# RWKV loop: a block's products split by what they need, POOL's later masks behind them, decay sums in halves of the array

## Chip, cores and metric

One core of a Trainium2 chip runs the whole program. The metric is the device time of one execution in microseconds (us), the median of several.

## What is computed

Two transformer blocks on 512 tokens of width 1024. The second block mixes tokens with differential attention and with a two-directional RWKV recurrence of 8 heads of 64 channels; the change is in that recurrence alone:

```python
def rwkv_scan(r, decay, k, v, kk, a, s0, reverse):
    def step(S, inp):
        r_t, w_t, k_t, v_t, kk_t, b_t = inp            # b = kk * a
        sa = jnp.einsum('bhvk,bhk->bhv', S, kk_t)
        S = (S * w_t[:, :, None, :] - sa[..., None] * b_t[:, :, None, :]
             + v_t[..., None] * k_t[:, :, None, :])
        return S, jnp.einsum('bhvk,bhk->bhv', S, r_t)
...
decay = jnp.exp(-jnp.exp(w))
a = jax.nn.sigmoid((a0 + al @ a2).astype(jnp.float32))
k_dir = k * (1.0 + (a - 1.0) * p['k_a'])
```

It runs over 256 context tokens and then 512 tokens, forwards and backwards.

## The kernel before

The recurrence is done in chunks of 64 tokens: 12 chunks (`NCH`), of which the first 4 are context (`main(n)` is true from chunk 4). Both directions go together; a tile has 128 partitions, that is two heads of 64 channels (`HEADS` are the two row halves), four such pairs per direction. Two chunks make a block of 128 tokens (6 blocks). All matmuls are float32; the profile counts two records for each.

The order of work is written out by hand for each engine, with semaphores between them. The loop runs over iterations n = -1 to 12. In iteration n the triangular system of chunk n is inverted in five levels (`lv` 0 to 4), while the state of chunk m = n - 1 is finished and the Gram matrices of chunk g = n + 1 are made. A level is: T product on TensorE (`t_level`), copy by ScalarE, XY product on TensorE (`xy_level`), `update` on VectorE (line 3066), once per direction. Work of the other chunks stands between ("aside" work of `t_level`):

- level 0: `kv`; level 1: `gram_l`, `sa`, `gram_lt`, then VectorE's `x_init` and `y_init` (lines 3048 and 3051) and POOL's addition of the identity (line 3139);
- level 2: `outputs`, `new_state`, VectorE's `state` (lines 3071 and 3075);
- level 3: `gram` B, evacuated by VectorE to GB (line 3058); POOL makes five masked copies of GB from it, one per level (`loff`, line 3125), for the T products of the next iteration;
- level 4: `gram` K, evacuated to GK.

Blocks are prepared ahead, one direction at levels 3 and 4 each. Odd iterations make the rates (`latents` on TensorE, lines 2747 and 2749, sigmoids on ScalarE), even ones the sums of log decay (`cums`, line 2757, four matmuls of 128x256 with a mask "sums" that keeps the two chunks apart) and ScalarE's exponentials (`exps`). From these VectorE makes the operands of the next Gram matrices (`products`, lines 3034 to 3044) with one multiplication by POOL (`kka`, line 3118) among them. `products(b, 0)` stands at the end of an even iteration, `products(b, 1)` behind level 0 of the odd iteration that follows; `gram_l` of level 1 waits for both (`prods`). Block b is prepared in iteration n = 2b - 2, block 0 ahead of the loop.

Of the kernel before, what the change touches and what calls it, by code (L numbers as in the profile page):

```python
# [16 lines left out]
ALU = mybir.AluOpType  # L17
# [3 lines left out]
P = 128  # L21
# [2662 lines left out]
def rwkv_loop(k):  # L2684
# [17 lines left out]
    YF = v(A_MIX, KD, S)  # L2702
    ident = [k.ident[h, h] for h in HEADS]
    sems = {n: k.sem(f"rwkv_{n}") for n in (
        "latent_done", "rated", "cums_done", "exps", "k_gain", "kka", "prods", "gram_l", "gram_lt", "gram_b", "gram_k", "x_init", "y_init",
        "gb", "gk", "loff", "eye", "t_done", "t_copied", "xy_done", "xy", "turned", "tok_copied", "kv_done", "kv_copied",
        "sa_done", "sa_copied", "s_done", "state", "y_done", "y_copied")}
    flat = lambda ap: ap.rearrange("p a b -> p (a b)")
# [33 lines left out]
    def tensor(k, pe):  # L2742
# [9 lines left out]

        def cums(b, d):
            wait("rated", prep(b, d))
            for f in range(4):
                o = 2048 + 256 * f
                mm = pe.matmul(k.psum[:, o:o + 256], SIG[d][:, f * P:(f + 1) * P], mask(k, "sums", 0, 256), start=True, stop=True)  # L2757
            mm.then_inc(sems["cums_done"], 1)

        def prepare(n, d):  # L2760
# [161 lines left out]
        for n in range(-1, NCH + 1):  # L2922
            m, g, live = n - 1, n + 1, 0 <= n < NCH
            for lv in range(LEVELS):
                aside = nothing
                if lv == 1 and g < NCH:
                    aside = gram_l(g)
                elif lv == 2 and m >= 0:
                    aside = outputs(m)
                elif lv == 3 and g < NCH:  # L2930
                    aside = gram(g, B, "gram_b")
                elif lv == 4 and g < NCH:
                    aside = gram(g, K, "gram_k")
                if live:
                    t_level(n, lv, aside)
                rest(aside)
                if lv == 0 and m >= 0:
                    aside = turn_kb(m) if m < NCH - 1 else nothing
                    kv(m, n, aside)
                    rest(aside)  # L2940
                if lv == 1:
                    aside = turn_v(n) if live else nothing
                    if m >= 0:
                        sa(m, aside)
                    rest(aside)
                if lv == 4:
                    prepare(n, 1)
                if live:
                    xy_level(n, lv)
                if lv == 1 and g < NCH:  # L2950
                    gram_lt(g)
                if lv == 2 and 0 <= m < NCH - 1:
                    new_state(m, n)
                if lv == 3:
                    if n == -1:
                        wait("exps", 2)
                    prepare(n, 0)

    def scalar(k, act):
        wait = lambda name, value: act.wait_ge(sems[name], value)  # L2960
# [5 lines left out]

        def exps(b, d):
            wait("cums_done", prep(b, d))
            cum = k.psum[:, 2048:3072].rearrange("p (f w c t) -> p f w c t", f=4, w=2, c=2)
# [52 lines left out]
    def vector(k, dve):  # L3022
        wait = lambda name, value: dve.wait_ge(sems[name], value)

        def products(b, d):
            n, tok = b % 2, block_tokens(b, d)
            at_tokens = lambda name: src[name][:, :, tok].rearrange("p f (c t) -> p f c t", c=2)
            rate = RATE[d].rearrange("p (f t) -> p f t", f=4)
            Kf, Bf = (x[n][d].rearrange("p f c t -> p f (c t)") for x in (K, B))
            ka = M[:, O_VEC + VCOL["k_a_2"]:O_VEC + VCOL["k_a_2"] + 4].unsqueeze(2).broadcast_to([P, 4, 2 * CH])  # L3030
            wait("exps", prep(b, d))
            if b >= 2:
                wait("tok_copied", 3 * (2 * b - 2))
            ins = dve.scalar_tensor_tensor(out=Kf, in0=rate, scalar=-1.0, in1=ka, op0=ALU.add, op1=ALU.mult)
            ins.then_inc(sems["k_gain"], 1)
            tile = AR[n][d]
            dve.tensor_tensor(tile[:, :, :, 0, :], tile[:, :, :, 0, :], at_tokens("KK"), ALU.mult)
            if main(2 * b):
                dve.tensor_tensor(tile[:, :, :, 1, :], tile[:, :, :, 1, :], at_tokens("R"), ALU.mult)
            wait("k_gain", prep(b, d))  # L3040
            k.dve.link(dve.scalar_tensor_tensor(out=Kf, in0=Kf, scalar=1.0, in1=src["K"][:, :, tok], op0=ALU.add, op1=ALU.mult))
            k.dve.link(dve.tensor_tensor(Kf, Kf, Bf, ALU.mult))
            wait("kka", prep(b, d))
            dve.tensor_tensor(Bf, rate, Bf, ALU.mult).then_inc(sems["prods"], 1)  # L3044
# [31 lines left out]
            ins.then_inc(sems["state"], 1)  # L3076

        dve.memset(ST[0], 0.0).then_inc(sems["state"], 1)
        for d in range(2):
            products(0, d)  # L3080
        for n in range(-1, NCH + 1):
            m, g, live = n - 1, n + 1, 0 <= n < NCH
            for lv in range(LEVELS):
                if lv == 3 and g < NCH:
                    wait("gram_b", g + 1)
                    evacuate(g, GB, 0, 0)
# [8 lines left out]
                    evacuate(g, GK, 1, 1).then_inc(sems["gk"], 1)  # L3095
                if live:
                    update(n, lv, 1)
                if lv == 0 and n >= 1 and exps_in(n - 1) is not None:
                    products(exps_in(n - 1), 1)
                if lv == 1 and g < NCH:  # L3100
                    x_init(g)
                if lv == 2 and m >= 0 and main(m) and second_visit(m):
                    wait("y_done", m - NCH_CTX + 1)
                    for d in range(2):
# [2 lines left out]
                if lv == 2 and 0 <= m < NCH - 1:  # L3107
                    state(m)
            if exps_in(n) is not None:
                products(exps_in(n), 0)  # L3110

    def pool(k, pool):
        wait = lambda name, value: pool.wait_ge(sems[name], value)

        def kka(b, d):
            wait("k_gain", prep(b, d))
            rate = RATE[d].rearrange("p (f t) -> p f t", f=4)
            pool.tensor_tensor(rate, rate, src["KK"][:, :, block_tokens(b, d)], ALU.mult).then_inc(sems["kka"], 1)

        def loff(g, lv):  # L3120
            if lv == 0:
# [7 lines left out]
        for d in range(2):  # L3129
            kka(0, d)  # L3130
        for n in range(-1, NCH):
            g = n + 1
            if n >= 1 and exps_in(n - 1) is not None:
                kka(exps_in(n - 1), 1)
# [7 lines left out]
            if exps_in(n) is not None:  # L3142
                kka(exps_in(n), 0)

    return Phase("rwkv_loop", tensor=tensor, vector=vector, scalar=scalar, pool=pool)

# [288 lines left out]
```

## Time and profile before

| | |
|---|---|
| median of 3 runs | 2701.26 us (2696.73 to 2702.88) |
| profiled execution: its time, its span | 2695.02 us, 2693.1 us |
| TensorE matmul busy, weight load busy | 2495.5 us (93%), 1935.5 us (72%) |
| VectorE, ScalarE, POOL busy | 1337.9, 510.6, 160.1 us |
| loop, 1797 to 2169 us: TensorE, VectorE, ScalarE, POOL busy | 288.23, 187.04, 121.26, 122.13 us |
| mean granted clock in the loop, in the span | 0.94, 0.967 |

Times in the rows are us from the start of the span. The ends of iterations are taken at the end of VectorE's last update: iteration 6 ends at 2016.92, 7 at 2049.50, 8 at 2078.59, 9 at 2110.38, 10 at 2136.67. A granted clock of 1.00 is 2.4 GHz, 0.50 is 1.2 GHz.

### The profile page before, as it was taken

To read this page: it belongs to the slowest core of one execution; us is meant where nothing else is said; L and a number is where in the kernel's file an instruction comes from. 1 tells how busy PE (TensorE), PEld (TensorE's weight loads), DVE (VectorE), ACT (ScalarE), POOL (GpSimd) and SP (SyncE) were. 2 spreads that over 40 slices of the span, in tenths; PEclk is the share of its full clock that TensorE was granted. 3 is DMA by queue.
4 is the path that set the end of the run, shared out by engine and by line. 5 is a ranking of instruction groups with operands and counts; after the bars stand their busy time and mean duration, and the time that the engine had idled before them with its cause. 6 is when DMAs were issued, how large, how long until landed. Compare 5 with 4: busy or idle time off the path is not lost.

```text
span 2693.1 us, 49099 instructions
## 1 busy us (share of the span) xinstructions
PE 2495.5 (93%) x21464; PEld 1935.5 (72%) x21464; DVE 1337.9 (50%) x2466; ACT 510.6 (19%) x1032; POOL 160.1 (6%) x118
## 2 busy tenths in 40 slices
PE   8989999999999999999999989978877798999997
PEld 5945888888686448888884744547777746888886
DVE  4625555523444346555333274734555435777523
ACT  1121110001004320010001053223333222122100
POOL 0000000000000000000000000004333200000000
PEclk9988999999999999999999989989999998999998
DMA  4323222234120032222333103100000023222132
GB/s 163 120 76 125 94 93 69 70 86 122 56 89 30 1 125 67 91 94 75 82 110 116 46 16 84 32 1 4 4 4 4 4 94 107 82 94 94 50 90 65
DMA packets 221182, 190.54 MB, mean 71 GB/s; under 512 B 8727, under 2 KB 219064, under 8 KB 220968
## 3 DMA queue, kind: packets, MB, share of 16 engines
q1 hardware_dynamic: 220674, 187.29, 22.3%
q8 instruction: 171, 2.80, 0.4%
q14 instruction: 43, 0.35, 0.0%
q10 hardware_dynamic: 294, 0.09, 0.0%
HBM read 185.25 MB, written 2.10 MB: 70 GB/s over the span
## 4 chain that ended last, share of the span: by engine, by line
PE 86%; DVE 7%; issue 2%; ACT 2%; SPq 1%; DMA 1%; POOL 1%; DVEq 0%; POOLq 0%; ACTq 0%
PE psum L1630 30%; PE psum L1840 14%; PE psum L512 8%; PE psum L1130 4%; PE psum L2673 4%; PE psum L1344 3%; PE psum L2680 3%; PE psum L1341 3%; PE psum L3218 2%; PE psum L542 2%; PE psum L1066 1%; PE psum L2270 1%; PE psum L2757 1%; PE psum L2252 1%; DVE sbuf L3066 1%
## 5 line engine op out<-in xcount | busy, mean ns | idle before, releaser
L1630 PE MATMUL psum<-sbuf 128*128 128x256 f32 x3696 | 805.5, 381 | 3.6 <-ACT sbuf L488 1.7
L1630 PEld LDWEIGHTS psum<-sbuf 128*128 128x128 f32 x3696 | 707.0, 191 | 101.7 <-issue 3.1
L1840 PE MATMUL psum<-sbuf 128*128 128x256 f32 x1848 | 403.9, 381 | 11.1 <-DVE sbuf L1858 5.5
L1840 PEld LDWEIGHTS psum<-sbuf 128*128 128x128 f32 x1848 | 352.9, 191 | 61.8 <-DVE sbuf L1858 6.3
L1714 DVE TENSOR_TENSOR sbuf<-sbuf,psum 128x256 f32<-128x256 f32 x462 | 177.9, 417 | 201.2 <-PE psum L1630 200.0
L512 PE MATMUL psum<-sbuf 128*128 128x512 f32 (+3 forms) x688 | 247.9, 519 | 4.3 <-DVEq L617 4.0
L2680 PE MATMUL psum<-sbuf 64*64 64x64 f32 x4992 | 204.1, 231 | 30.0 <-issue 14.3
L2673 PE MATMUL psum<-sbuf 64*64 64x64 f32 (+1 forms) x4544 | 178.1, 232 | 48.7 <-DVE sbuf L3044 31.5
L512 PEld LDWEIGHTS psum<-sbuf 128*128 128x128 f32 (+2 forms) x688 | 129.4, 189 | 115.5 <-issue 103.4
L2680 PEld LDWEIGHTS psum<-sbuf 64*64 64x64 f32 x4992 | 179.3, 142 | 42.9 <-issue 34.8
L2673 PEld LDWEIGHTS psum<-sbuf 64*64 64x64 f32 x4544 | 162.8, 140 | 54.3 <-DVE sbuf L3044 32.7
L427 POOL TENSOR_TENSOR sbuf<-sbuf 128x512 f32<-128x512 f32 x30 | 37.8, 1279 | 1925.3 <-DVE sbuf L413 1925.1
L1876 DVE TENSOR_TENSOR sbuf<-sbuf,psum 128x256 f32<-128x256 f32 x84 | 34.2, 419 | 229.0 <-PE psum L1840 228.6
L3066 DVE TENSOR_TENSOR sbuf<-sbuf,psum 128x512 f32<-128x512 f32 (+1 forms) x120 | 73.5, 630 | 122.4 <-PE psum L2673 122.2
L1130 PE MATMUL psum<-sbuf 128*128 128x512 f32 x256 | 117.0, 607 | 0.0
L1650 ACT ACTIVATE sbuf<-sbuf 128x512 f32<-128x512 f32 x44 | 27.7, 630 | 399.7 <-DVE sbuf L1714 399.7
L1130 PEld LDWEIGHTS psum<-sbuf 128*128 128x128 f32 x256 | 48.0, 195 | 53.1 <-issue 53.1
L1344 PE MATMUL psum<-sbuf 128*128 128x256 f32 x392 | 85.4, 379 | 0.0
L1700 DVE TENSOR_TENSOR sbuf<-sbuf 128x512 f32<-128x512 f32 x66 | 44.5, 690 | 81.2 <-PE psum L1630 67.1
L1344 PEld LDWEIGHTS psum<-sbuf 128*128 128x128 f32 x392 | 74.2, 190 | 11.3 <-issue 1.3
L1178 DVE TENSOR_REDUCE sbuf<-psum 128x1 f32<-128x256 f32 (+3 forms) x80 | 36.8, 460 | 87.7 <-PE psum L1066 52.0
L3125 POOL TENSOR_TENSOR sbuf<-sbuf 128x512 f32<-128x512 f32 x60 | 74.2, 1273 | 67.9 <-DVE sbuf L3058 67.9
(280 smaller groups left out, 2719.5 us busy)
## 6 DMA issues: line engine op xcount, KB each, us to landing
sbuf<-in_w_mod_dram SPq DMA_DIRECT2D x24, 1024.0 KB, 5.2
sbuf<-in_w_ffn_gate_dram SPq DMA_DIRECT2D x22, 1024.0 KB, 5.3
sbuf<-in_w_ffn_up_dram SPq DMA_DIRECT2D x22, 1024.0 KB, 7.8
sbuf<-in_w_ffn_down_dram SPq DMA_DIRECT2D x32, 704.0 KB, 6.0
sbuf<-in_w_up_dram SPq DMA_DIRECT2D x22, 1024.0 KB, 7.0
sbuf<-in_w_out_dram SPq DMA_DIRECT2D x12, 1024.0 KB, 7.5
sbuf<-in_w_in_dram SPq DMA_DIRECT2D x12, 1024.0 KB, 5.4
sbuf<-in_w_down_dram SPq DMA_DIRECT2D x16, 704.0 KB, 6.1
```

The source lines that it names most:

```text
L512: mm = pe.matmul(bank, w[:, q, c0:c0 + m], rhs(k0 + q), start=start and q == 0, stop=stop and q == kc - 1)
L542: mm = pe.matmul(bank, act_chunk(q), w[:, q, :], start=q == 0, stop=q == kc - 1)
L1130: mm = pe.matmul(bank_of(b), tiles[b // 2][:, q, (b % 2) * P:(b % 2) * P + P], MIX[:, q, :], start=q == 0, stop=q == KD - 1)
L1341: mm = pe.matmul(self.bank(p)[:, t * P:(t + 1) * P], x[:, q, t * P:(t + 1) * P], w[:, q, :], start=q == 0, stop=q == 3)
L1344: mm = pe.matmul(self.bank(p), w[:, q, :], x[:, q, :], start=q == 0, stop=q == 3)
L1630: mm = pe.matmul(bank, w[:, q, :], rhs[:, q, :], start=q == 0, stop=q == 3)
L1714: dve.tensor_tensor(out, base, bank_of(u, p, t), ALU.add).then_inc(s["added"], 1)
L1840: mm = pe.matmul(bank_of(g, p), wt[:, q, :], rhs_of[p][:, q, :], start=q == 0, stop=q == UNITS - 1)
L2673: mm = pe.matmul(out[h], lhsT[h], rhs[h], start=start, stop=stop)
L2680: mm = pe.matmul(out[o], lhsT[h], rhs[h], start=start, stop=stop)
L3066: dve.tensor_tensor(xy, xy, new, ALU.subtract).then_inc(sems["xy"], 1)
L3125: pool.tensor_tensor(split(LOFF[lv]), split(GB[g % 2][:, :, 0, :]), both_level(lv), ALU.mult).then_inc(sems["loff"], 1)
```

## The change

- `cums` becomes eight matmuls: for each of four feature groups one per chunk, with the 64 rows of that chunk as contraction, into bank 4 for the first chunk and bank 5 for the second. ScalarE reads them in the new layout.
- TensorE's first `prepare` moves from behind the XY product of level 3 to ahead of it.
- `products` is split. `rate_products` (gain of the key, and the product of rate and KK that POOL made) goes to level 0 of the even iteration for both directions, `key_products` to level 1, the rest of the first direction to the head of level 4, the rest of the second to the end of the even iteration. Ahead of the loop, block 0's rate and key products stand before its exponentials are waited for.
- POOL no longer multiplies; its mask copies of levels 2 to 4 in an even iteration wait for the block's last product (`prods`).

```diff
         def cums(b, d):
             wait("rated", prep(b, d))
+            sums = mask(k, "sums", 0, 256).rearrange("p (w c t) -> p w c t", w=2, c=2)
             for f in range(4):
-                o = 2048 + 256 * f
-                mm = pe.matmul(k.psum[:, o:o + 256], SIG[d][:, f * P:(f + 1) * P], mask(k, "sums", 0, 256), start=True, stop=True)
+                for c, rows in enumerate(HEADS):
+                    mm = pe.matmul(k.bank[4 + c][:, f * P:(f + 1) * P], SIG[d][rows, f * P:(f + 1) * P], sums[rows, :, c, :],
+                                   start=True, stop=True)
             mm.then_inc(sems["cums_done"], 1)
...
+                if lv == 3:
+                    if n == -1:
+                        wait("exps", 2)
+                    prepare(n, 0)
                 if lv == 4:
                     prepare(n, 1)
                 if live:
...
-                if lv == 3:
-                    if n == -1:
-                        wait("exps", 2)
-                    prepare(n, 0)
...
-            wait("exps", prep(b, d))
             if b >= 2:
                 wait("tok_copied", 3 * (2 * b - 2))
-            ins = dve.scalar_tensor_tensor(out=Kf, in0=rate, scalar=-1.0, in1=ka, op0=ALU.add, op1=ALU.mult)
-            ins.then_inc(sems["k_gain"], 1)
-            tile = AR[n][d]
+            for d in range(2):
+                rate, Kf, _ = of_block(b, d)
+                wait("rated", prep(b, d))
+                dve.scalar_tensor_tensor(out=Kf, in0=rate, scalar=-1.0, in1=ka, op0=ALU.add, op1=ALU.mult).then_inc(sems["k_gain"], 1)
+            for d in range(2):
+                rate, _, _ = of_block(b, d)
+                wait("k_gain", prep(b, d))
+                dve.tensor_tensor(rate, rate, src["KK"][:, :, block_tokens(b, d)], ALU.mult).then_inc(sems["kka"], 1)
+
+        def key_products(b):
+            for d in range(2):
+                _, Kf, _ = of_block(b, d)
+                wait("k_gain", prep(b, d))
+                dve.scalar_tensor_tensor(out=Kf, in0=Kf, scalar=1.0, in1=src["K"][:, :, block_tokens(b, d)], op0=ALU.add,
+                                         op1=ALU.mult).then_inc(sems["k_made"], 1)
+
+        def products(b, d):
...
+            wait("exps", prep(b, d))
             dve.tensor_tensor(tile[:, :, :, 0, :], tile[:, :, :, 0, :], at_tokens("KK"), ALU.mult)
             if main(2 * b):
                 dve.tensor_tensor(tile[:, :, :, 1, :], tile[:, :, :, 1, :], at_tokens("R"), ALU.mult)
-            wait("k_gain", prep(b, d))
-            k.dve.link(dve.scalar_tensor_tensor(out=Kf, in0=Kf, scalar=1.0, in1=src["K"][:, :, tok], op0=ALU.add, op1=ALU.mult))
+            wait("k_made", prep(b, d))
             k.dve.link(dve.tensor_tensor(Kf, Kf, Bf, ALU.mult))
             wait("kka", prep(b, d))
             dve.tensor_tensor(Bf, rate, Bf, ALU.mult).then_inc(sems["prods"], 1)
...
             for lv in range(LEVELS):
+                if lv == 4 and exps_in(n) is not None:
+                    products(exps_in(n), 0)
...
-                if lv == 0 and n >= 1 and exps_in(n - 1) is not None:
-                    products(exps_in(n - 1), 1)
+                if lv == 0 and exps_in(n) is not None:
+                    rate_products(exps_in(n))
                 if lv == 1 and g < NCH:
                     x_init(g)
+                if lv == 1 and exps_in(n) is not None:
+                    key_products(exps_in(n))
...
             if exps_in(n) is not None:
-                products(exps_in(n), 0)
+                products(exps_in(n), 1)
...
                 for lv in range(LEVELS):
+                    if lv == 2 and exps_in(n) is not None:
+                        wait("prods", prep(exps_in(n), 1))
                     loff(g, lv)
```

VectorE's row before, from the end of iteration 6 (level 4's evacuations and updates) to the level-1 update of iteration 7:

```order
1251 L3058 TENSOR_TENSOR sbuf<-psum,sbuf 128x512
1252 L3066 TENSOR_TENSOR sbuf<-sbuf,psum 128x256
1253 L3058 TENSOR_TENSOR sbuf<-psum,sbuf 128x512
1254 L3066 TENSOR_TENSOR sbuf<-sbuf,psum 128x256
1255 L3034 SCALAR_TENSOR_TENSOR sbuf<-sbuf 128x512
1256 L3037 TENSOR_TENSOR sbuf<-sbuf 128x8x64
1257 L3039 TENSOR_TENSOR sbuf<-sbuf 128x8x64
1258 L3041 SCALAR_TENSOR_TENSOR sbuf<-sbuf 128x512
1259 L3042 TENSOR_TENSOR sbuf<-sbuf 128x512
1260 L3044 TENSOR_TENSOR sbuf<-sbuf 128x512
1261 L3066 TENSOR_TENSOR sbuf<-sbuf,psum 128x2x256 x2
1262 L3034 SCALAR_TENSOR_TENSOR sbuf<-sbuf 128x512
```

The same place after the change, in whose numbering L3058 to L3064 are the four products, L3078 the evacuation and L3086 the update:

```order
1250 L3058 TENSOR_TENSOR sbuf<-sbuf 128x8x64
1251 L3060 TENSOR_TENSOR sbuf<-sbuf 128x8x64
1252 L3062 TENSOR_TENSOR sbuf<-sbuf 128x512
1253 L3064 TENSOR_TENSOR sbuf<-sbuf 128x512
1254 L3078 TENSOR_TENSOR sbuf<-psum,sbuf 128x512
1255 L3086 TENSOR_TENSOR sbuf<-sbuf,psum 128x256
1256 L3078 TENSOR_TENSOR sbuf<-psum,sbuf 128x512
1257 L3086 TENSOR_TENSOR sbuf<-sbuf,psum 128x256
1258 L3058 TENSOR_TENSOR sbuf<-sbuf 128x8x64
1259 L3060 TENSOR_TENSOR sbuf<-sbuf 128x8x64
1260 L3062 TENSOR_TENSOR sbuf<-sbuf 128x512
1261 L3064 TENSOR_TENSOR sbuf<-sbuf 128x512
```

Two sets of six between the updates have become one set of four ahead of level 4's evacuations and one of four behind its updates.

The rest of them stands in levels 0 to 1 of iteration 6 after the change (L3040 key gain, L3044 rate times KK, L3068 and L3071 the starts of X and Y, L3050 the key product):

```order
1236 L3086 TENSOR_TENSOR sbuf<-sbuf,psum 128x2x256 x2
1237 L3040 SCALAR_TENSOR_TENSOR sbuf<-sbuf 128x512 x2
1238 L3044 TENSOR_TENSOR sbuf<-sbuf 128x512 x2
1239 L3086 TENSOR_TENSOR sbuf<-sbuf,psum 128x2x256 x2
1240 L3068 TENSOR_TENSOR sbuf<-psum,sbuf 128x512
1241 L3071 TENSOR_TENSOR sbuf<-psum,sbuf 128x512
1242 L3050 SCALAR_TENSOR_TENSOR sbuf<-sbuf 128x512 x2
1243 L3086 TENSOR_TENSOR sbuf<-sbuf,psum 128x2x256 x2
```

Four instructions have come between the updates of level 0 and level 1, and two between the start of Y and the updates of level 2.

## Rows read from the trace of the kernel before

**Rows 1.** Waits in the loop: us in total, times, longest us.

```profile
PEld psum L2680 <- issue: 34.8, 50, 2.3
...
PE psum L2673 <- DVE sbuf L3044: 31.5, 6, 6.8
```

**Rows 2.** Stretches of iterations 7, 8, 9 and 10, one row each.

```profile
core 0: us, PE busy (x) PEld busy (x) DVE busy (x) ACT busy (x) POOL busy (x), PEclk, DMA share, GB/s
...
2016.92:2049.50 32.58, 24.64 (x948) 23.30 (x948) 20.84 (x32) 10.43 (x23) 10.68 (x8) 0.90 0.02 4
2049.50:2078.59 29.09, 24.77 (x944) 22.31 (x944) 11.12 (x21) 11.45 (x27) 9.67 (x7) 1.00 0.02 4
2078.59:2110.38 31.79, 23.01 (x928) 21.80 (x928) 21.29 (x34) 6.50 (x16) 9.58 (x7) 0.84 0.02 4
2110.38:2136.67 26.29, 21.18 (x928) 19.67 (x928) 11.68 (x21) 6.49 (x16) 8.55 (x7) 1.00 0.02 4
```

**Rows 3.** Timeline of VectorE, iteration 6's level 3 to iteration 7's level 1.

```profile
2007.59 0.69 DVE L3058 TENSOR_TENSOR sbuf<-psum,sbuf 128x512 f32<-128x512 f32 x1 [0.27 <-PE psum L2673]
...
2016.51 0.41 DVE L3066 TENSOR_TENSOR sbuf<-sbuf,psum 128x256 f32<-128x256 f32 x1
...
2018.04 1.76 DVE L3039 TENSOR_TENSOR sbuf<-sbuf 128x512 f32<-128x512 f32 x1
...
2021.16 0.69 DVE L3044 TENSOR_TENSOR sbuf<-sbuf 128x512 f32<-128x512 f32 x1
...
2027.29 0.69 DVE L3044 TENSOR_TENSOR sbuf<-sbuf 128x512 f32<-128x512 f32 x1
2032.61 1.44 DVE L3066 TENSOR_TENSOR sbuf<-sbuf,psum 128x512 f32<-128x512 f32 x2 [4.64 <-PE psum L2673]
```

**Rows 4.** Timeline of ScalarE around the first exponentials of iteration 6.

```profile
2007.81 1.28 ACT L2972 ACT_TABLE_LOAD   x1
2011.12 0.60 ACT L2972 ACTIVATE sbuf<-psum 128x512 f32<-128x512 f32 x1 [2.02 <-PE psum L2757]
```

**Rows 5.** Chain that ended last: latents of iteration 5, cums of iteration 6.

```profile
1980.60 0.31 PE psum L2747
...
1981.35 0.34 PE psum L2749 x3
...
2009.16 1.92 PE psum L2757 x8
...
2012.99 1.92 PE psum L2757 x8
```

**Rows 6.** Timeline of POOL: identity in iteration 0, masks and product in 6.

```profile
1828.41 2.37 POOL L3139 TENSOR_TENSOR sbuf<-sbuf 128x1024 f32<-128x1024 f32 x1 [4.29 <-DVE sbuf L3051]
...
2009.56 6.18 POOL L3125 TENSOR_TENSOR sbuf<-sbuf 128x512 f32<-128x512 f32 x5 [7.79 <-DVE sbuf L3058]
2017.60 1.65 POOL L3118 TENSOR_TENSOR sbuf<-sbuf 128x512 f32<-128x512 f32 x1 [1.87 <-DVE sbuf L3034]
```

**Rows 7.** Stretches of 2 us in iteration 7, columns as in rows 2.

```profile
2024.00:2026.00 2.00, 0.00 (x0) 0.00 (x0) 2.00 (x3) 0.00 (x0) 1.38 (x1) 1.00 0.00 0
...
2028.00:2030.00 2.00, 1.97 (x72) 1.97 (x76) 0.00 (x0) 0.51 (x2) 0.00 (x0) 0.50 0.03 8
```

**Rows 8.** Timeline of VectorE, level 2 of iteration 0; levels 0, 1, 2 of 8.

```profile
1829.17 1.38 DVE L3066 TENSOR_TENSOR sbuf<-sbuf,psum 128x512 f32<-128x512 f32 x2 [0.91 <-PE psum L2673]
...
2052.66 0.69 DVE L3066 TENSOR_TENSOR sbuf<-sbuf,psum 128x512 f32<-128x512 f32 x1 [3.15 <-PE psum L2673]
...
2058.38 1.29 DVE L3066 TENSOR_TENSOR sbuf<-sbuf,psum 128x512 f32<-128x512 f32 x2 [3.45 <-PE psum L2673]
...
2064.81 1.28 DVE L3066 TENSOR_TENSOR sbuf<-sbuf,psum 128x512 f32<-128x512 f32 x2 [3.94 <-PE psum L2673]
```

**Rows 9.** Start of the loop, timelines of VectorE and of TensorE.

```profile
1802.29 0.69 DVE L3034 SCALAR_TENSOR_TENSOR sbuf<-sbuf 128x512 f32<-128x512 f32 x1 [10.90 <-ACT sbuf L2976]
...
1811.09 1.65 PE L2673 MATMUL psum<-sbuf 64*64 64x64 f32 x26 [6.78 <-DVE sbuf L3044]
```

More of the change, by code:

```diff
@@ L2704, in rwkv_loop @@
     sems = {n: k.sem(f"rwkv_{n}") for n in (
-        "latent_done", "rated", "cums_done", "exps", "k_gain", "kka", "prods", "gram_l", "gram_lt", "gram_b", "gram_k", "x_init", "y_init",
+        "latent_done", "rated", "cums_done", "exps", "k_gain", "kka", "k_made", "prods", "gram_l", "gram_lt", "gram_b", "gram_k", "x_init", "y_init",
         "gb", "gk", "loff", "eye", "t_done", "t_copied", "xy_done", "xy", "turned", "tok_copied", "kv_done", "kv_copied",
@@ L2968, in exps @@
             wait("cums_done", prep(b, d))
-            cum = k.psum[:, 2048:3072].rearrange("p (f w c t) -> p f w c t", f=4, w=2, c=2)
+            cum = k.psum[:, 2048:3072].rearrange("p (c f w t) -> p f w c t", c=2, f=4, w=2)
             incl, excl = cum[:, :, 0], cum[:, :, 1]
@@ L3023, in vector, with of_block, rate_products @@
         wait = lambda name, value: dve.wait_ge(sems[name], value)
-        def products(b, d):
-            n, tok = b % 2, block_tokens(b, d)
-            at_tokens = lambda name: src[name][:, :, tok].rearrange("p f (c t) -> p f c t", c=2)
+        def of_block(b, d):
+            n = b % 2
             rate = RATE[d].rearrange("p (f t) -> p f t", f=4)
             Kf, Bf = (x[n][d].rearrange("p f c t -> p f (c t)") for x in (K, B))
+            return rate, Kf, Bf
+        def rate_products(b):
             ka = M[:, O_VEC + VCOL["k_a_2"]:O_VEC + VCOL["k_a_2"] + 4].unsqueeze(2).broadcast_to([P, 4, 2 * CH])
-            wait("exps", prep(b, d))
             if b >= 2:
                 wait("tok_copied", 3 * (2 * b - 2))
-            ins = dve.scalar_tensor_tensor(out=Kf, in0=rate, scalar=-1.0, in1=ka, op0=ALU.add, op1=ALU.mult)
-            ins.then_inc(sems["k_gain"], 1)
-            tile = AR[n][d]
+            for d in range(2):
[13 more added lines that the diff above has]
+        def products(b, d):
+            rate, Kf, Bf = of_block(b, d)
+            at_tokens = lambda name: src[name][:, :, block_tokens(b, d)].rearrange("p f (c t) -> p f c t", c=2)
+            tile = AR[b % 2][d]
+            wait("exps", prep(b, d))
             dve.tensor_tensor(tile[:, :, :, 0, :], tile[:, :, :, 0, :], at_tokens("KK"), ALU.mult)
@@ L3078, in vector @@
         dve.memset(ST[0], 0.0).then_inc(sems["state"], 1)
+        rate_products(0)
+        key_products(0)
         for d in range(2):
@@ L3109, in vector @@
             if exps_in(n) is not None:
-                products(exps_in(n), 0)
+                products(exps_in(n), 1)
     def pool(k, pool):
         wait = lambda name, value: pool.wait_ge(sems[name], value)
[L3115 to L3118, printed above, removed]
         def loff(g, lv):
@@ L3128, in pool @@
             [P, 2, 4, CH])
-        for d in range(2):
-            kka(0, d)
         for n in range(-1, NCH):
             g = n + 1
-            if n >= 1 and exps_in(n - 1) is not None:
-                kka(exps_in(n - 1), 1)
             if g < NCH:
```

2 lines of the change are left out of this document (removed).

## Prediction

> **What bounds the kernel now.** I first read the times and the page, then the waits of the RWKV loop, then one stretch per iteration, then the instructions of iterations 6 to 8 engine by engine. The loop is about 370 of 2695 us; the change touches nothing else, so all of the effect must come from there. In the loop no engine is full: TensorE and VectorE hand work to each other at every level (T product, ScalarE copy, XY product, VectorE update). Two waits stand out [rows 1]: TensorE waits six times for the last product of a block, 31.5 us in all, up to 6.8 us at once; and it stops for "issue" (nothing in the profile released it), 34.8 us on its weight-load side in 50 stops.
>
> The stretches show who pays [rows 2]. Iterations 7 and 9 (odd: a block's second set of products runs in them) take 32.58 and 31.79 us; iterations 8 and 10 take 29.09 and 26.29 us. Iterations 9 and 10 do the same work except for the products: 5.50 us apart. In iteration 6 VectorE ends the last update at 2016.92, then does block 4's first products until 2021.8, the next two updates, and the second products until 2027.98; the next XY update comes at 2032.61 [rows 3]. In iteration 8 the same three kinds of update come at 2052.66 and 2058.38 with VectorE idle 3.15 and 3.45 us before them [rows 8]. From the last update (iteration 7's ended at 2049.50, the boundary in [rows 2]) to the level-1 update it is 8.9 us there, and 15.7 us where the products stand between. The 6.8 us are two things: TensorE has nothing to do while VectorE multiplies, and its granted clock falls with it. It was 1.00 in 2024 to 2026 and 0.50 in 2028 to 2030, that is 1.2 instead of 2.4 GHz, after a stretch in which it did nothing [rows 7].
>
> **The change, part by part.**
>
> *Products taken out of the chain.* Per block and direction, before: six VectorE instructions (five in the two context blocks) and one on POOL. After: the two that need only the rate, with POOL's product now VectorE's, go to level 0 of the even iteration, the key product to level 1, the three or four that need the exponentials to level 4 (first direction) and behind it (second). VectorE spends 0.6 to 0.7 us on each.
>
> Odd iterations gain. What is left behind the last update is one direction's four products: 0.6+0.6+0.7+0.7 = 2.6 us, and POOL's masks of levels 2 to 4 are made to wait for them, so nothing holds the port. The idle time there is 3.15 us [rows 8], so it is covered; without cover each 0.6 us would lie on the path. Gain per odd iteration: 5.50 us from iterations 9 and 10. For iteration 7: iteration 8 has two cums of 1.92 us and iteration 7 two latents of 1.09 us (1980.60 to 1981.69) [rows 5], so a free iteration 7 should take 29.09 - 2 x 0.83 = 27.4, gain 5.2. I take 5.3 for all five odd iterations: -26.5. Bounds: nothing taken off for cums, (32.58-29.09 = 3.5) in four of them and 5.5 in the ninth: -19.5; the whole distance 15.7 - 8.9 in each: -34.
>
> *Rate and key products in gaps.* Four instructions, 2.5 us, against the 3.45 us of idle time behind level 0's updates: hidden from iteration 4 on. The two key products come right behind Y's start, just when POOL adds the identity (2.37 us in the row of iteration 0) [rows 6]. These collide: when POOL's 1.65 us product started at 2017.60, VectorE's instruction of 2018.04 took 1.76 instead of 0.69 us, and ended 0.55 us after POOL did [rows 3, 6]. So the second key product ends about 0.6+2.37+0.6 = 3.6 us after Y's start. In iteration 8 the next update is idle for 3.94 us: hidden. In iteration 0 it is idle for 0.91 us [rows 8]: first key product 1828.2 to 1828.9, POOL to 1831.25, second to 1831.8, so the update of 1829.17 moves by 2.6 us. With up to 0.7 for the rate products there (POOL is still at its masks) and 1.0 for iteration 2, where new_state on TensorE covers most: +4.3.
>
> *Level 3 and 4 of even iterations*, worked through for iteration 6. TensorE ends gram B at about 2007.6 (VectorE's row of 2007.59). Cums now stands here: the same 2048 columns, but in halves of 64 rows with a bank each. Latents, which already feed two separate row ranges into two banks, push 2 x 512 columns in one and 8 x 128 in the other in 1.09 us together, so they overlap; I take 1.0 instead of 1.92 (bounds 0.96 and 1.92). Then the XY product's first half (2008.95), update 0.65, GB evacuation 0.6, update 0.65: 2010.85. GB is whole at 2010.25, and gram K with the T product, 1.91 us between the two cums [rows 5], ends at 2012.2 instead of 2012.99; cums and XY product of level 4 end at 2013.8 instead of 2015.6. So TensorE is 1.8 us early. ScalarE: table load ends 2009.1 [rows 4], four exponentials 0.5 apart: 2010.8.
>
> VectorE gives this back. It now meets products(b, 0), four instructions, at 2010.85, ahead of GK's evacuation and both updates. POOL gets GB at 2010.3 and makes two masks of 1.24 us (6.18 for five [rows 6]). With two SBUF inputs VectorE waits for each as above: 2.6 us of work and 2 x 1.24 less the 0.5 already gone by: end 2015.3. Then evacuation 0.6, update 0.34, evacuation 0.6, update 0.41: 2017.3, against 2016.92 before. So +0.4 per even iteration, +2.0. Bounds: no collision, -1.5 each (-7.5); POOL's masks put between every pair cannot cost more, since only two are let through before the new wait.
>
> The Trainium skill bears on this (SBUF — State Buffer, Who interferes with whom): an instruction of VectorE with two SBUF inputs and a GpSimd instruction that reads SBUF never share the port pair; the later one waits for the whole of the other. By it the collision is certain; without it the last number would be 2015.5 instead of 2017.3. The rows of 2017.60 and 2018.04 agree.
>
> *POOL's new wait.* Behind it stand masks 2 to 4 (3.7 us). They start about 2.7 us after the last update and end at +6.4; the T product of level 2 needs the first of them after the level-1 update, at +8.9 at the earliest. Costs nothing; its cover is 2.5 us or more.
>
> *Start.* Before, products began only after the first exponentials, at 1802.29, and TensorE's gram waited 6.78 us for the tenth of them, until 1811.09 [rows 9]. Four of ten are now done while ScalarE and TensorE are still at the first sums, the first sums are 1.9 us shorter (at half clock), and no POOL instruction stands between (about 2 x 1.07): 1802.3 - 1.9 + 6 x 0.65 + 0.7 of waiting for the second exponentials gives 1805. Gain 6.
>
> **Sum.** -26.5 + 4.3 + 2.0 - 6.0 = -26.2 us on the profiled execution's 2695.02: 2668.8. That execution lies 6.2 us under the median of the runs shown (2701.26), so on the median's scale it is 2675; I give 2674.
>
> **Rivals.**
> 1. *The port costs nothing, or the odd iterations give the whole distance.* Even iterations then keep 1.5 us each (-7.5 for +2.0) and odd ones up to 6.8. Against: the 1.76 us row, and iteration 9 to 10, which gave 5.5 of its 6.7. Time 2650 to 2662. Chance 0.09.
> 2. *Issue stops take the freed time.* TensorE runs through an odd iteration at half clock for some 5 us now; at full clock it uses up instructions faster, and stops of about 0.7 us (34.8/50 [rows 1]) come more often. Three or four more per odd iteration: +2.5 each, +12.5. For: such stops stand in the fast iterations. Against: iteration 10 has them and is the measure I used. Time 2687. Chance 0.13. In a sentence of its own: the Trainium skill (Runtime: NRT & Kernel Launch, Instruction fetch mechanics) says that instructions are refilled in blocks of 256 ahead of use and that this is mostly hidden; by that this rival would be nothing.
> 3. *The clock falls in the new gap.* In level 4 of an even iteration TensorE is done at 2013.8 and VectorE delivers at 2016.3: 2.5 us with nothing to do. The clock fell after such a stretch in the odd iteration, where nothing ran in 2024 to 2026 [rows 7]. If it falls in each of five gaps and 5 us then run at half speed, +2.5 each: 2687. Chance 0.1.
> 4. *Slower.* The same fall, lasting: then the T product, the kv and sa products of the next iteration run at half clock and TensorE's next gaps keep it down. It turns the sign from 5.2 us lost per pair of iterations, 10.5 us at half clock; at 15 us of half clock it is +37 - 26 = 2712. Against: in all odd iterations so far the clock came back within some 6 us of steady work. Chance 0.04.
> 5. *Nothing to be measured*, for instance because the second products at the end of the even iteration still hold up the level-0 update and the early ones level 1 (2.6 us each time, 13) and rival 2 comes too: about 2699. Chance 0.04.
>
> The forecast, 2664 to 2684, has 0.6. The range 2659 to 2689 takes in rivals 2 and 3 and leaves out most of 1, and 4 and 5. A measurement of this kernel tells 0.2% (5.4 us): faster by more 0.91, within 0.04, slower 0.05.
>
> **What would show each step.** In odd iterations, the granted clock stays at 1.00 and TensorE no longer waits for the products' last line; the distance last update to level-1 update is about 9 us. Each cums takes about 1 us. In even iterations one or two of the four products at level 4 last 1.2 to 1.8 us instead of 0.7, and the evacuation of GK comes at the end of them. The second key product takes over 2 us, and only iterations 0 and 2 feel it. Iteration 7 takes 27.4, 9 takes 26.3, 6 about 30.6. The forecast is wrong if odd iterations stay above 29 us or even ones rise above 32.

## The result, and the profile after

| | before | after |
|---|---|---|
| median of 4 runs | 2699.24 us | 2676.47 us (2674.92 to 2680.07) |
| ratio | | 0.9923, 95% interval 0.9906 to 0.9939 |
| profiled execution: its time, its span | 2695.02, 2693.1 us | 2680.07, 2678.3 us |
| first latents to last update of iteration 11 | 368.9 us | 360.6 us |

A second comparison, with 5 runs of the change, gave 0.9930 (0.9918 to 0.9942). The change is faster by 0.7 to 0.8%, about 20 us; 2674 had been forecast, against 2676.5.

The stall that the change removes is gone from the iterations. The profile's stretches of iterations 7, 8, 9 and 10 after the change, cut as in [rows 2] at VectorE's last updates:

```profile
core 0: us, PE busy (x) PEld busy (x) DVE busy (x) ACT busy (x) POOL busy (x), PEclk, DMA share, GB/s
...
2008.01:2038.26 30.25, 23.33 (x948) 21.55 (x948) 13.71 (x23) 10.55 (x23) 11.13 (x9) 1.00 0.02 4
2038.26:2069.89 31.63, 23.75 (x960) 21.53 (x960) 21.07 (x30) 11.67 (x27) 6.75 (x4) 1.00 0.02 4
2069.89:2097.33 27.44, 21.00 (x928) 19.69 (x928) 14.26 (x26) 6.50 (x16) 10.01 (x8) 1.00 0.02 4
2097.33:2125.31 27.98, 22.50 (x928) 21.30 (x928) 11.78 (x21) 6.51 (x16) 8.56 (x7) 0.94 0.02 5
```

Iterations 7 and 9 have fallen from 32.58 and 31.79 us to 30.25 and 27.44, and the granted clock in them from 0.90 and 0.84 to 1.00. Iterations 8 and 10 are longer than in [rows 2], by 2.5 and 1.7 us; iteration 10 has no products and no sums, so nothing was edited in it. In the second profiles of both kernels (below) iteration 8 takes 30.7 us before and 30.3 after, so nothing of its excess is left; iteration 10 takes 27.1 and 28.9, the same difference again, and what lengthens it is open.

VectorE in iteration 6, from the level-1 updates to the level-1 update of iteration 7 (L3050 key products, L3078 evacuation, L3086 update, L3058 to L3064 the products that need exponentials), answers to [rows 3]:

```profile
1989.12 0.68 DVE L3071 TENSOR_TENSOR sbuf<-psum,sbuf 128x512 f32<-128x512 f32 x1
1989.72 3.44 DVE L3050 SCALAR_TENSOR_TENSOR sbuf<-sbuf 128x512 f32<-128x512 f32 x2
1993.09 0.68 DVE L3086 TENSOR_TENSOR sbuf<-sbuf,psum 128x512 f32<-128x512 f32 x1
...
1998.22 0.69 DVE L3078 TENSOR_TENSOR sbuf<-psum,sbuf 128x512 f32<-128x512 f32 x1 [0.43 <-PE psum L2673]
1999.96 0.69 DVE L3086 TENSOR_TENSOR sbuf<-sbuf,psum 128x512 f32<-128x512 f32 x1 [1.04 <-PE psum L2673]
...
2001.76 1.39 DVE L3058 TENSOR_TENSOR sbuf<-sbuf 128x512 f32<-128x512 f32 x1
2003.07 1.75 DVE L3060 TENSOR_TENSOR sbuf<-sbuf 128x512 f32<-128x512 f32 x1
2004.74 0.68 DVE L3062 TENSOR_TENSOR sbuf<-sbuf 128x512 f32<-128x512 f32 x1
2005.46 0.69 DVE L3064 TENSOR_TENSOR sbuf<-sbuf 128x512 f32<-128x512 f32 x1
2006.07 0.68 DVE L3078 TENSOR_TENSOR sbuf<-psum,sbuf 128x512 f32<-128x512 f32 x1
...
2007.60 0.41 DVE L3086 TENSOR_TENSOR sbuf<-sbuf,psum 128x256 f32<-128x256 f32 x1
...
2009.85 0.69 DVE L3064 TENSOR_TENSOR sbuf<-sbuf 128x512 f32<-128x512 f32 x1
2012.58 1.29 DVE L3086 TENSOR_TENSOR sbuf<-sbuf,psum 128x512 f32<-128x512 f32 x2 [2.04 <-PE psum L2673]
2017.52 0.69 DVE L3086 TENSOR_TENSOR sbuf<-sbuf,psum 128x512 f32<-128x512 f32 x1 [3.65 <-PE psum L2673]
```

Three things are to be seen. The last update of iteration 6 ends at 2008.01 and the level-1 update of iteration 7 comes at 2017.52, 9.5 us later instead of 15.7. At level 4 two of the four products are stretched, to 1.39 and 1.75 us, and the evacuation of GK waits for all four. The second key product waits for POOL's identity: 3.44 us for two. POOL's timeline at the same places:

```profile
1989.94 2.67 POOL L3156 TENSOR_TENSOR sbuf<-sbuf 128x1024 f32<-128x1024 f32 x1 [10.49 <-DVE sbuf L3071]
2001.33 2.95 POOL L3146 TENSOR_TENSOR sbuf<-sbuf 128x512 f32<-128x512 f32 x2 [8.71 <-DVE sbuf L3078]
```

The two masks take 2.95 us, where five took 6.18 [rows 6]: mask, product, mask, product. So the engines take turns, one instruction each, even though POOL's second mask was ready from the start.

What took part of the gain back is seen in TensorE's waits. First iteration 9 before (2078.59 to 2110.38), then iteration 9 after (2069.89 to 2097.33); the columns are us in total, times, longest us:

```profile
PE psum L2673 <- DVE sbuf L3044: 5.0, 1, 5.0
PE psum L2680 <- DVE sbuf L3066: 2.6, 4, 1.7
PE psum L2673 <- issue: 0.9, 2, 0.7
...
PE psum L2680 <- issue: 0.2, 1, 0.2
```

```profile
PE psum L2680 <- issue: 2.4, 2, 1.4
PE psum L2673 <- issue: 2.0, 3, 1.0
PE psum L2819 <- issue: 1.1, 1, 1.1
```

The wait of 5.0 us for the products is gone, and "issue" (stops in which TensorE waited for nothing that the profile shows) has gone from 1.1 to 5.5 us.

### The profile page after: what moved, and what is told of

The parts are those of the page before. It is cut to its first block, busy times and chain, and to the rows that moved or that the text cites. A ratio compares the mean times of both kernels' runs of the same rounds, so it can differ in the third digit from the quotient of the medians.

```text
span 2678.3 us, 49291 instructions
## 1 busy us (share of the span) xinstructions
PE 2486.2 (93%) x21560; PEld 1929.4 (72%) x21560; DVE 1350.4 (50%) x2478; ACT 512.7 (19%) x1032; POOL 144.5 (5%) x106
## 4 chain that ended last, share of the span: by engine, by line
PE 86%; DVE 6%; issue 3%; ACT 2%; SPq 1%; POOL 1%; DMA 0%; DVEq 0%; POOLq 0%; ACTq 0%
PE psum L1630 30%; PE psum L1840 14%; PE psum L512 8%; PE psum L1130 4%; PE psum L2680 4%; PE psum L2673 3%; PE psum L1344 3%; PE psum L1341 3%; PE psum L3235 2%; PE psum L542 2%; PE psum L1066 1%; DVE sbuf L3086 1%; PE psum L2270 1%; PE psum L2252 1%; PE psum L1109 1%
## 5 line engine op out<-in xcount | busy, mean ns | idle before, releaser
L2680 PEld LDWEIGHTS psum<-sbuf 64*64 64x64 f32 x4992 | 175.5, 139 | 62.7 <-issue 53.7
L2673 PE MATMUL psum<-sbuf 64*64 64x64 f32 (+1 forms) x4544 | 177.0, 230 | 21.7 <-issue 15.4
L2673 PEld LDWEIGHTS psum<-sbuf 64*64 64x64 f32 x4544 | 160.4, 138 | 28.0 <-issue 18.3
L3086 DVE TENSOR_TENSOR sbuf<-sbuf,psum 128x512 f32<-128x512 f32 (+1 forms) x120 | 73.1, 630 | 114.4 <-PE psum L2673 114.2
```

Of the source, the lines that this page charges most:

```text
L2673: mm = pe.matmul(out[h], lhsT[h], rhs[h], start=start, stop=stop)
L2680: mm = pe.matmul(out[o], lhsT[h], rhs[h], start=start, stop=stop)
L3086: dve.tensor_tensor(xy, xy, new, ALU.subtract).then_inc(sems["xy"], 1)
```

## Where the gain went: terms against two profiles of each kernel

Both kernels were profiled a second time (`c_before`, `c_after`). All entries are us. The two numbers under before and after are the two profiles of that kernel, and the difference is that of their means. Iterations are cut as above; "start" is from the first latents to the end of iteration 0.

| stretch | before | after | difference | forecast |
|---|---|---|---|---|
| start | 49.2, 49.7 | 51.9, 51.8 | +2.3 | -6.0 + 3.3 + 0.4 |
| odd iterations 1 to 9 | 158.0, 159.5 | 139.5, 138.2 | -19.9 | -26.5 |
| even iterations 2 to 8 | 112.6, 116.7 | 117.7, 116.4 | +2.5 | +1.0 + 1.6 |
| iterations 10 and 11 | 49.1, 51.1 | 51.6, 51.1 | +1.2 | 0 |
| loop | 368.9, 377.0 | 360.6, 357.4 | -13.9 | -26.2 |
| before and behind the loop | 2324.2, 2322.7 | 2317.7, 2316.9 | -6.2 | 0 |
| span | 2693.1, 2699.7 | 2678.3, 2674.3 | -20.1 | -26.2 |

Two profiles of one kernel differ by up to 4 us in a row (even iterations before), so differences of 1 or 2 us are not to be leaned on. The total came into the range partly by luck: the loop's gain was overestimated by 12 us, and 6 us outside of it, which had not been forecast, made up half of that.

## Experiments

**Second profiles.** Nothing edited.

> The kernel before, unchanged, for a second profile. The profiled change gained only 8.3 us inside the loop (first latents to last update: 368.9 us before, 360.6 after), while the medians are 22.8 us apart. Theory 1 (the loop's length varies between executions): a second profile gives a loop that differs from 368.9 by 4 us or more. Theory 2 (the loop is steady and other phases vary): within 2 us of 368.9.

> The changed kernel, unchanged, for a second profile and a closer ratio. Expected ratio 0.990 to 0.994 by what was measured. Theory 1 (clock at the start of the loop, at 1.2 GHz until 1819 in the first profile, differs between executions): the loop is 3 us or more shorter than 360.6. Theory 2: again 359 to 362 us, with the low clock at the start.

Measured: 2701.47 us (one run) and 2676.76 us. The loop took 377.0 and 357.4 us: it varies by 8 us between two executions of the kernel before, by 3 of the change. One profile's 8.3 us was too little, as theory 1 had it for the kernel before. For the change neither theory fits whole: the loop was 3.2 us shorter, as theory 1 had it, but the low clock at the start came again (0.67 as in the first profile), as theory 2 had it.

**e1_old_sums.** The sums of log decay as before and back behind level 3's XY product, products as in the change.

```diff
             for f in range(4):
-                for c, rows in enumerate(HEADS):
-                    mm = pe.matmul(k.bank[4 + c][:, f * P:(f + 1) * P], SIG[d][rows, ...], sums[rows, :, c, :], ...)
+                o = 2048 + 256 * f
+                mm = pe.matmul(k.psum[:, o:o + 256], SIG[d][:, f * P:(f + 1) * P], mask(k, "sums", 0, 256), start=True, stop=True)
...
                 if lv == 2 and 0 <= m < NCH - 1:
                     new_state(m, n)
+                if lv == 3:
+                    ...
+                    prepare(n, 0)
```

> The changed kernel with the sums of log decay as before: four matmuls of full height behind level 3's XY product. If halving and moving them is worth what the sum says (0.9 us for each of two per even iteration, of which level 4 gives all back), ratio to before 0.991 to 0.995, that is 0 to 5 us slower than the change, most of it at the start. If issue stops count (the halves add 32 TensorE instructions per even iteration), it is as fast or faster than the change by 1 to 3 us.

Measured: 0.9915 (0.9903 to 0.9927), median 2671.2: about 5 us faster than the change in the medians, not slower, with intervals that overlap. Loop 355.5 us. The start is 50.2 us, where the change has 51.8. In iteration 6 the products of level 4 wait 2.9 us for the exponentials and then all take 0.7 us, since POOL has finished its two masks.

**e2_sums_alone.** The mirror image: `cums`, its place and ScalarE's layout as in the change, all products as before.

> The kernel before with the sums in halves and moved, products as before. By my sum, sums are 1.0 instead of 1.9 us, on TensorE's path in even iterations, and nothing collides at level 4: 1.5 us per even iteration and 2 at the start, 8 to 10 us faster (0.9965). If the next link (ScalarE's table load and exponentials, VectorE's evacuation) is what ends there, under 3 us (0.999).

Measured: 1.0011 (1.0002 to 1.0019), slower than before by up to 5 us; loop 379.8 us, against 368.9 and 377.0. So the sums' part of the change gains nothing by itself, and all that the change gains comes with the products and POOL's wait. The 1.5 us per even iteration and the 2 us at the start that were expected of the sums are refuted.

**e8_halves_old_place.** The change, with `prepare(n, 0)` again behind level 3's XY product (the move in the diff undone), the sums in halves.

> The changed kernel with the sums in halves, but the first direction's again behind level 3's XY product. The old sums in the old place were about 4 us faster than the change. If the place is what costs (VectorE's level-3 updates wait for the XY product behind the sums, and the exponentials come early enough to bring the products into POOL's masks), this is 3 to 5 us faster than the change, ratio 0.9915. If the halves with their 32 more instructions cost, it is as slow as the change, 0.993.

Measured: 0.9909 (0.9895 to 0.9922), median 2671.9, loop 352.3 us. This run differs from e1 in the halves alone, and the two are equal; it differs from the change in the place alone. So the place ahead of the XY product is what seems to cost, not the halves; the intervals of both runs just overlap that of the change. VectorE at levels 3 and 4 of iteration 6 here:

```profile
1996.52 0.69 DVE L3078 TENSOR_TENSOR sbuf<-psum,sbuf 128x512 f32<-128x512 f32 x1 [0.71 <-PE psum L2673]
1997.13 0.68 DVE L3086 TENSOR_TENSOR sbuf<-sbuf,psum 128x512 f32<-128x512 f32 x1
...
2000.29 1.25 DVE L3058 TENSOR_TENSOR sbuf<-sbuf 128x512 f32<-128x512 f32 x1 [1.28 <-ACT sbuf L2978]
2001.46 0.68 DVE L3060 TENSOR_TENSOR sbuf<-sbuf 128x512 f32<-128x512 f32 x1
...
2004.91 0.41 DVE L3086 TENSOR_TENSOR sbuf<-sbuf,psum 128x256 f32<-128x256 f32 x1
```

From the first evacuation to the end of the last update it is 8.80 us, against 9.79 in the change (1998.22 to 2008.01). In the change the level-3 update waits 1.04 us for an XY product that stands behind the sums, and the first two products meet POOL's masks; here the update follows at once and only one product is stretched.

**e5_products_at_end.** The first direction's products behind level 4's updates.

```diff
-                if lv == 4 and exps_in(n) is not None:
-                    products(exps_in(n), 0)
...
             if exps_in(n) is not None:
-                products(exps_in(n), 1)
+                for d in range(2):
+                    products(exps_in(n), d)
```

> The changed kernel with the first direction's products taken out of level 4 and put behind level 4's updates, ahead of the second direction's. Level 4 loses its 4.5 us of products and port waits. Behind it stand now 5.2 us of products (and up to 2.5 of port waits) against 3.15 us of idle time. If the level-4 collision costs what the sum says (0.4 net, 1.8 for the port), then this is 0 to 2 us slower per even iteration, 0 to 10 us slower than the change; if TensorE's idle gap at level 4 (with the clock's fall that follows it in iterations 3 and 5) is the larger cost, up to 8 us faster.

Measured: 0.9910 (0.9897 to 0.9923), median 2672.9, loop 352.7 us: four products at level 4, with their waits for POOL, cost more than four more behind the updates. The run does not part the collision from the products' own 2.6 us. In iteration 6 the same distance falls from 9.79 to 8.14 us (1995.00 to 2003.14), and the next level-0 update comes 4.98 us after the last update instead of 4.57: 1.65 us gained, 0.4 lost.

**e9_old_sums_at_end.** The edits of e1 and e5 together.

> The changed kernel with the sums as before and the first direction's products behind level 4's updates: the two variants that were each 4 to 5 us faster than the change together. If they save different things 0.989 to 0.990; if both save the same collision at level 4, 0.991.

Measured: 0.9929 (0.9916 to 0.9942), loop 356.3 us: no better than the change, a miss of both readings. The traces of iteration 6 suggest why. With the sums late, level 4's products stand mostly in time that is idle anyway: from the first evacuation to the end of the last update it is 9.95 us with them there (e1) and 9.60 us without (e9). Moved behind the updates, they push the next level-0 update from 4.28 to 4.98 us after the last one. It was not tested further.

**e4_key_first.** `key_products` ahead of `x_init` instead of behind it.

> The changed kernel with the two key products ahead of the start of X instead of behind the start of Y, so that they no longer meet POOL's addition of the identity. They took 3.44 us for two in every even iteration; apart they should take 1.3. By my sum that is on the path in iterations 0 and 2 alone: 3 to 4 us faster than the change. By the profile after (the level-2 update follows at once in iterations 0, 2, 4, 6 and 8) all five gain 1 to 2 us: 5 to 9 us. If TensorE's issue stops take it back: 0 to 2 us.

Measured: 0.9932 (0.9919 to 0.9945), as the change; loop 357.4 us. VectorE's rows there:

```profile
1987.67 1.29 DVE L3050 SCALAR_TENSOR_TENSOR sbuf<-sbuf 128x512 f32<-128x512 f32 x2
...
1992.10 0.69 DVE L3086 TENSOR_TENSOR sbuf<-sbuf,psum 128x512 f32<-128x512 f32 x1 [1.95 <-PE psum L2673]
```

The pair takes 1.29 instead of 3.44 us, and the level-2 update waits 1.95 us for TensorE where it had followed at once. The collision was real, and removing it this way gains nothing in the total. The edit does not price the collision alone, since X and Y now start 1.2 us later, behind the key products. In iteration 6 the two cancel: the second level-2 update starts 7.4 us after the first level-1 update, against 7.1 in the change. At the start they do not: it takes 48.9 us in this profile, 2.9 less than in the change, yet the loop is as long as in the change's second profile (357.4).

**e3_no_pool_wait.** POOL's wait removed; each mask still waits for its own inputs.

```diff
-                    if lv == 2 and exps_in(n) is not None:
-                        wait("prods", prep(exps_in(n), 1))
```

> The changed kernel without POOL's wait for the products at level 2, so that masks 2 to 4 run as soon as their own inputs are there. If the port pair is what the wait protects, all eight products of levels 4 and after collide with masks: up to three masks more of 1.24 us, so 2.5 to 3.7 us per even iteration, 12 to 18 us slower than the change (ratio 0.997 to 1.0). If level 0 of the next iteration has room for it, under 3 us.

Measured: 0.9982 (0.9972 to 0.9993), median 2692.5, 15.8 us slower than the second median of the change. VectorE at level 4 of iteration 6, and POOL:

```profile
2007.74 1.39 DVE L3058 TENSOR_TENSOR sbuf<-sbuf 128x512 f32<-128x512 f32 x1
2009.05 1.75 DVE L3060 TENSOR_TENSOR sbuf<-sbuf 128x512 f32<-128x512 f32 x1
2010.73 1.75 DVE L3062 TENSOR_TENSOR sbuf<-sbuf 128x512 f32<-128x512 f32 x1
2012.52 1.64 DVE L3064 TENSOR_TENSOR sbuf<-sbuf 128x512 f32<-128x512 f32 x1
```

```profile
2007.30 7.97 POOL L3146 TENSOR_TENSOR sbuf<-sbuf 128x512 f32<-128x512 f32 x5 [10.09 <-DVE sbuf L3078]
```

Now all four are stretched, by 0.7 to 1.1 us each, turn and turn about with five masks. By the ratios (0.9982 against 0.9930) the wait is worth three quarters of what the whole change gains.

**e7_start_waits.** Ahead of the loop, `wait("exps", 1)` in front of `rate_products(0)`.

> The changed kernel with one thing undone: ahead of the loop VectorE again waits for block 0's first exponentials before any of its products. In both profiles of the change the start (first latents to the end of iteration 0) took 51.8 us against 49.2 and 49.7 before, although the products end 5 us sooner, with the clock at 1.2 GHz nearly throughout. If the shorter stall has kept the clock low, waiting again makes the start no longer than 52, and the kernel equal within 2 us. If the earlier products are worth what the sum says, 4 to 6 us slower than the change.

Measured: 0.9919 (0.9905 to 0.9933), median 2675.6, equal to the change; the start took 54.0 us instead of 51.8, 2 more than the reading of a clock kept down by the shorter stall allowed, and the clock stayed low in it (0.66). So it is not the earlier products that keep the clock down. They are worth some 2 us in the profile and nothing that the medians show.

**e6_filler and e10_filler_wide.** TensorE work added at an idle place, behind level 4's XY product in the five even iterations with products.

```diff
+                if lv == 4 and exps_in(n) is not None:
+                    for _ in range(12):       # e10: range(2)
+                        by_head(pe, k.bank[1][:, 508:512], T[:, 0, :], T[:, 0, 0:4])   # e10: 256 columns
```

> The changed kernel with 24 tiny matmuls (4 columns, into a part of a bank that nothing reads; work added, results unchanged) on TensorE behind level 4's XY product of the five even iterations with products, where it is idle for some 2.5 us. They are 96 TensorE instructions each time. 
> The changed kernel with TensorE work at the place of the tiny matmuls that cost 6 us, for about as long (four matmuls of 64 rows and 256 columns, 0.9 us, into a part of a bank that nothing reads; work added, results unchanged) but in 16 instructions instead of 96. If the number of instructions cost the 6 us, this is equal to the change within 2 us (0.993). If TensorE's time there cost it, 4 to 6 us slower again (0.995).

Measured: 0.9952 (0.9940 to 0.9963), median 2684.2, loop 364.2 us; and 0.9937 (0.9923 to 0.9950), median 2679.6, loop 360.1 us. Against the change's 2676.8 that is +7.4 and +2.8. So 96 instructions per time cost 4.6 us more in the medians than 16. But the two fillers are not equally long: in iteration 6 the tiny matmuls keep TensorE busy for 1.5 us and the wide ones for 1.0, which in five iterations can make 2.5 of the 4.6 us. The wide filler's +2.8 also lies between what was expected of either reading, and the intervals of the ratios overlap. A limit in the supply of TensorE's instructions is a hint here, not shown. As to the clock's dips, iterations 3 and 5 have 0.95 and 0.94 with the tiny filler and 1.00 with the wide one; iteration 3 has 1.00 in e7 too, without a filler, so single profiles do not settle it.

## Why the prediction was right, and where it was not

*The stall of the odd iterations: right in kind, a third too large.* TensorE no longer waits for a block's last product in the iterations (ahead of them it waits once, 3.3 us instead of 6.8), and from the last update to the level-1 update of iterations 1, 3, 5, 7 and 9 it takes 8.9, 10.2, 8.6, 9.5 and 9.2 us, where 9 had been said. The failing term is "I take 5.3 for all five odd iterations": it measures 4.0, 19.9 us in all, just above the small end of its bounds (19.5). Behind the level-1 update the odd iterations have become longer (iteration 9: 16.1 before, 18.2 after). Rival 2 offers a reason: it was priced as another case, 12.5 us on top, and may in part have been this one. TensorE's issue waits in the loop were 30.9 and 39.2 us in the two profiles before, 45.5 and 43.3 after. That they grew, by 9.4 us in the means, is read from the traces; that they took back what is missing is not shown, since e1 has 49.3 us of them and a loop shorter than the change's, and their cause is open. Of the prediction's own signs, "wrong if odd iterations stay above 29 us" came true in one of five: iteration 7 takes 30.2 and 29.2 us in the two profiles, where 27.4 had been said.

*Rival 3, the clock.* It came too, seldom: the granted clock is 0.94 or 0.95 in iterations 3, 5 and 10 of the first profile and 3 and 9 of the second, and 0.99 to 1.00 in the others behind iteration 0. In all, a few us (an estimate from the stretches' clocks).

*Level 4 of even iterations: right for iteration 6.* The working gave products ending at 2015.3 and +0.4 us; the distance from gram B's first evacuation to the last update went from 9.33 to 9.79 us, +0.46, with the two port waits as said. The Trainium skill's rule on the port pair (SBUF — State Buffer, Who interferes with whom) is borne out by three runs: 1.39 and 1.75 us in the change, four stretched products without POOL's wait, 1.29 us for two key products once they no longer meet the identity. The sums in halves took 1.09 us instead of 1.92, where 1.0 was taken. But the step "So TensorE is 1.8 us early" led nowhere: e2 gains nothing by it, and e8 without the early place is 5 us faster in the medians.

*POOL's new wait: "costs nothing".* Nearly so: TensorE's weight loads wait for masks for 3.2 and 2.6 us in the whole loop, in stops of up to 0.6 us, against 0.9 and 1.2 before and 0.5 without the wait (e3). The reverse, what it saves, wasn't in the sum and is 16 us.

*Key products.* Right in size (3.44 for 3.6 us). The +2.6 for iteration 0 is borne out by e4's profile, whose start is 2.9 us shorter; in the medians nothing of the +4.3 is found.

*The start: wrong sign.* The gain of 6 was expected and +2.3 measured together with iteration 0. The products did what was said: TensorE's first gram came 15.3 us behind the first latents (1803.59) instead of 20.5, 5.1 us earlier. Then the clock took most of it. From the start of X to iteration 0's first update it is 12.8 us in the change, where it is 8.9 before; it is 12.8 in all ten profiles with sums in halves, e2's with the old products among them, and 8.9 in all four with full-height sums. These are VectorE's rows in the change, then in e1 (whose L3066 and L3084 are the start of X and the update):

```profile
1805.61 0.69 DVE L3068 TENSOR_TENSOR sbuf<-psum,sbuf 128x512 f32<-128x512 f32 x1 [2.07 <-PE psum L2673]
...
1818.42 0.69 DVE L3086 TENSOR_TENSOR sbuf<-sbuf,psum 128x512 f32<-128x512 f32 x1 [4.04 <-PE psum L2673]
```

```profile
1803.83 0.69 DVE L3066 TENSOR_TENSOR sbuf<-psum,sbuf 128x512 f32<-128x512 f32 x1 [1.98 <-PE psum L2673]
...
1812.78 1.28 DVE L3084 TENSOR_TENSOR sbuf<-sbuf,psum 128x512 f32<-128x512 f32 x2 [2.72 <-PE psum L2673]
```

The rest of iteration 0, from that first update to the last, grew from 17.8 to 21.7 us, 3.9 where 3.3 + 0.4 had been said for it. So of the failing term, the gain of 6 at the start, 5.1 us were there and 3.9 were lost to the clock. Stretches of 2 us at the start of the loop, of the change and then of e1, which has the sums as before:

```profile
1799.00:1801.00 2.00, 1.28 (x13) 0.99 (x10) 1.17 (x2) 0.67 (x2) 0.00 (x0) 0.50 0.00 0
...
1811.00:1813.00 2.00, 2.00 (x31) 1.78 (x30) 0.00 (x0) 1.09 (x2) 2.00 (x2) 0.50 0.00 0
...
1817.00:1819.00 2.00, 2.00 (x74) 2.00 (x70) 0.58 (x1) 0.45 (x2) 0.00 (x0) 0.50 0.04 8
```

```profile
1796.00:1798.00 2.00, 1.39 (x6) 1.25 (x7) 1.38 (x3) 0.56 (x2) 0.00 (x0) 1.00 0.00 0
...
1809.00:1811.00 2.00, 1.88 (x38) 1.62 (x34) 0.76 (x2) 0.72 (x2) 2.00 (x3) 1.00 0.00 0
```

With full-height sums the clock rises to 2.4 GHz at the end of the first of them; with halves, which keep TensorE busy for 2.08 instead of 3.78 us, it stays at 1.2 GHz until 1819. In all fourteen profiles the split is clean: the mean clock of the start is 0.80 to 0.83 in the four with full-height sums, 0.66 to 0.69 in the ten with halves. The forecast had let the clock fall in idle time only and never asked what brings it back. The length of the whole start does not follow the clock alone: e8, with halves in the old place, has a clock of 0.66 and takes 49.8 us, no longer than e1's 50.2. The halves let X start 1.6 us earlier than in e1 and lose 3.9 behind it, and e8 wins that back in the rest of iteration 0 (19.8 us against 22.3). So the +2.3 us are the sum of several terms, of which the clock is the largest.

*Outside the loop.* 6 us that no edit explains; the phases there are the same instructions. This part takes 2316.6 to 2321.8 us in the eleven profiles of the change and its variants, and 2321.4 to 2324.2 in the three with the products as before. So it differs by 5 us between kernels that are the same there, and part of the 6 us may be that scatter. Behind the loop it goes with the time at the low clock: in the first profiles 35.4 us before and 27.3 after, at half speed 4.1 us, where that part is 4.2 us shorter. Why is open.

## What to carry to other kernels

Price a freed engine by what it runs into next: the nearest iteration without the stall promised 5.3 us, and the real ones gave 4.0, while TensorE's stops without a visible cause grew. Where VectorE's instructions take both inputs from SBUF and POOL reads SBUF too, the two took turns instruction by instruction here; keeping POOL's later, not yet needed work back was worth 16 us, more than any single reordering that was tried. Test the parts of a bundled change apart: three variants of this one with one part undone or moved are 4 to 6 us faster than it in their medians (0.9909 to 0.9915 against 0.9930, intervals overlapping), and two of them together are not.

## What was not expected of the hardware

Cutting a piece of work into halves of the array kept the clock down here. The first sums of the loop, 3.8 us of full-height matmuls at 1.2 GHz, were followed by 2.4 GHz in four of four profiles; the same sums in halves of 64 rows, 2.1 us, in none of ten. Whether it is the shorter time or the half height was not tested. Being busy did not by itself bring the clock up here: in the change TensorE was busy without a break from 1808 to 1819, with matmuls of 33 and 64 of the array's 128 rows, and the granted clock stayed at 0.50 in every microsecond of it. At the start the low clock cost 3.9 us between the start of X and the first update, and the halves had saved 1.6.
